# Expert rows of two groups scattered into one PSUM tile and added once; the crowded branch moved ahead of the last rounding

## Chip, cores and metric

The kernel runs on one core of one Trainium2 chip. The metric is the device time of one launch in microseconds (us); the kernel before was run three times: 2159.14, 2161.22 and 2164.48 us, a median of 2161.22.

## The reference, cut to what matters

The program is one step of a four-layer transformer trunk on 384 tokens (128 context, 256 latent) of width 1024. Each layer has a token mixer (gated delta rule, grouped-query attention, latent attention, gated delta rule), a layer norm, a mixture of experts, and a layer norm. The change is in the mixture of experts alone:

```python
scores = sigmoid(t @ router_w); sel = scores + router_b
best_group = argmax(sum of the two best sel of each group of 4)    # 4 groups of 4 experts
e_idx = the two best experts within best_group; w = scores at e_idx, divided by their sum
hid = silu(t @ w_gate[e]) * (t @ w_up[e])                          # 256 wide, 16 experts
out = sum over e of (hid * combine[:, e]) @ w_down[e]
x   = layer_norm(ALPHA * x + (1 + gate) * out)
```

Each token uses experts of one group only. All is float32.

## The kernel before, in words

**Tiling.** A group's tokens are gathered into a tile of 128 rows by a matmul with a 0/1 matrix (`e_pick`), its four experts are computed on this tile, and the result (128 rows of 1024) is put back to the 384 token positions by a matmul with another 0/1 matrix (`e_put`), feature tile by feature tile: eight tiles (`ft` 0 to 7) of 128 features by 384 tokens. If any group has more than 128 tokens, the rest is computed in extra blocks behind a branch on a flag (`flags[0:1, 0, 2:3]`); with these inputs that arm isn't run, but each of TensorE, VectorE and ScalarE loads the flag and branches once per layer.

**Precision.** Float32 products are made of rounded parts (float32r): ScalarE copies a weight piece to a rounded `e_whi` (`split_high`, by L1722), VectorE subtracts to get the remainder `e_wlo` (`split_low`, L2857), and TensorE runs three matmuls per product: hi by hi, hi by lo, lo by hi (`split_products`, L1515, L1518, L1519). Expert weights stream from HBM in units of 1 MB into a ring of eight; a unit is two pieces, an expert six pieces (four gate and up, two down). The split parts have three buffers (`SPLITS`).

**The plan.** `MOE_STEPS` is the order on TensorE, written out once and used in each layer: for x = 0 to 15 the steps U(x), the gate and up products of expert x; D(x-2), the down product of expert x-2, which accumulates a group's four experts in PSUM banks 3 and 4; T(x-1), the transposes of its hidden rows (bank 2); and at some x the gathers G of the second pair of groups, the pair's weights W, and the scatters S. `MOE_FOLLOW` is derived from it: the order in which ScalarE and VectorE follow (P is the splits of a piece, u the silu and product of U, t the transposed hidden rows' rounding, y the rounding of a finished group's rows, s the additions of a scatter). A step's work on ScalarE and VectorE is placed behind the splits of the second piece of the next U or D.

**Scatter and addition.** When group j is done, ScalarE rounds its rows into `e_yhi` and VectorE makes the remainder `e_ylo` (`y_high`, `y_low`, L2870), in two halves. A step S(j, q) is two feature tiles (`scatter_piece`): each is two matmuls of 128x384 into one PSUM bank (L1545 with `e_yhi`, L1546 with `e_ylo`), and then VectorE adds the tile, times the gate, into the residual `bufx` (`scattered`, L2876) in two instructions, one for the 128 context columns and one for the 256 latent ones. Per layer: 4 groups x 8 tiles x 2 = 64 matmuls and 64 additions. The four steps of groups 0, 1 and 2 are in the plan at x = 6 and 7, 10 and 11, 14 and 15, two at each x; those of group 3 come last, behind D of the last expert. Banks 5 and 6 take turns for groups 0 to 2; group 3 has 6, 0, 1, 2. A tile's matmuls wait until the bank's last tile is added. `put_back(j)` (L2834) makes the 0/1 matrix of group j in one of two buffers; it runs for groups 2 and 3 after the additions of groups 0 and 1.

**The branch.** Before the last group's scatter each engine runs `crowded_blocks`: load the flag (L1564 on TensorE, L2173 on ScalarE, L2882 on VectorE), compare and branch (L1565, L2174, L2884), and in the arm taken here only increments of semaphores (from L1597, L2207, L2916), which stand for the blocks left out. On ScalarE and VectorE that is behind the rounding of group 3; on TensorE it is behind its last down product. Then TensorE scatters, VectorE adds, and the column sums of the layer norm (L812) follow the additions tile by tile.

`bufh` holds the mixer's and experts' input; in the expert stage its first 1024 columns are free unless a block of a crowded group uses them, the next 1024 hold `e_sg` and `e_hid`, and the last 1024 are free.

## Time and profile before

| What | Value |
|---|---|
| median of three runs | 2161.22 us |
| profiled execution | 2164.33 us, its span 2162.5 us |
| TensorE matmuls busy | 2007.7 us, 93% |
| VectorE busy | 1335.3 us, 62% |
| ScalarE busy | 1027.7 us, 48% |
| `e_wlo` split on VectorE (L2857) | 384 of 1220 ns |
| additions into `bufx` on VectorE (L2876) | 256 of 408 ns |

In the views, PE is TensorE's matmuls and PEld its weight loads, DVE is VectorE, ACT ScalarE, SP the queue that issues the loads; a q behind the name is the engine's sequencer. A row of a timeline gives the start in us, the duration in us, engine, line, operation, the tiles written and read, and in brackets how long the engine was idle before it and what ended that; adjacent instructions of one kind are merged with their count. A row by stretch gives the stretch, its length, the busy us (and the number of instructions) of PE, PEld, DVE, ACT and POOL, then TensorE's mean granted clock as a share of full speed, the DMA share and GB/s. Matmuls overlap: one of 128x384 reads 0.34 us, and the next starts 0.17 to 0.18 us after it.

### The profile page before, as it was taken

Reading aid. Unit: us, or ns where it says so; the run is one execution under the profiler, and the core shown is the slowest. Engines: PE = TensorE matmul, PEld = TensorE weight load, DVE = VectorE, ACT = ScalarE, POOL = GpSimd, SP = SyncE. Lnnn points to the kernel's source line nnn. Section 1 sums busy time; section 2 is a strip of 40 time slices with the busy share of each in tenths; the row PEclk is TensorE's granted clock in tenths of the full one; section 3 lists DMA queues with packets and bytes.
Section 4 is the critical chain, followed back from the end, with each engine's and each line's share of the span. In section 5 each row is a group of like instructions: output and inputs, shape, how many; then the busy total and the mean of one; then the engine's idle time right before and its main releaser. Section 6 shows DMA issues by size and latency. Waiting matters only on the chain.

```text
span 2162.5 us, 45013 instructions
## 1 busy us (share of the span) xinstructions
PE 2007.7 (93%) x18880; PEld 1401.7 (65%) x18881; DVE 1335.3 (62%) x2625; ACT 1027.7 (48%) x1779; POOL 246.4 (11%) x363
## 2 busy tenths in 40 slices
PE   6999999899998999899899999998999999989996
PEld 3666666557775675687665666776566666646774
DVE  2666666448895341789722326898666666538896
ACT  3344344227773340676523315766444444327774
POOL 1422222110001000100010001000322232100000
PEclk9999999999999999999999999999999999999999
DMA  9244333257885244788632356888311121125880
GB/s 396 90 160 149 123 131 136 107 184 284 287 315 190 98 169 158 263 305 302 225 109 101 117 198 232 300 304 293 113 53 66 46 70 46 46 81 188 282 308 31
DMA packets 56911, 381.21 MB, mean 176 GB/s; under 512 B 6400, under 2 KB 10624, under 8 KB 12144
## 3 DMA queue, kind: packets, MB, share of 16 engines
q1 hardware_dynamic: 51696, 373.00, 48.3%
q10 hardware_dynamic: 4608, 4.20, 0.6%
q8 instruction: 158, 2.59, 0.5%
q0 software_dynamic: 384, 0.89, 0.1%
q14 instruction: 65, 0.53, 0.1%
HBM read 373.96 MB, written 4.10 MB: 175 GB/s over the span
## 4 chain that ended last, share of the span: by engine, by line
PE 74%; DVE 16%; ACT 5%; issue 3%; DMA 1%; DVEq 0%; SPq 0%; ACTq 0%
PE ps L851 15%; DVE e_wlo L2857 7%; PE ps L1515 5%; PE ps L1519 5%; PE ps L1518 5%; PE ps L801 4%; PE ps L777 4%; PE ps L757 4%; PE ps L1304 3%; PE ps L992 3%; DVE bufx L2876 3%; PE ps L812 2%; PE ps L1471 2%; ACT e_whi L1722 2%; PE ps L1404 2%
## 5 line engine op out<-in xcount | busy, mean ns | idle before, releaser
L2857 DVE TENSOR_TENSOR e_wlo<-ring,e_whi 128x1024 fp32r<-128x1024 f32 x384 | 455.0, 1220 | 70.1 <-ACT e_whi L1722 68.6
L1722 ACT ACTIVATE e_whi<-ring 128x1024 fp32r<-128x1024 f32 x384 | 402.5, 1060 | 114.7 <-PE ps L1519 111.9
L851 PE MATMUL ps<-bufh,ring 128*128 128x384 f32 x1024 | 390.2, 503 | 2.0 <-ACT scratch L1722 0.6
L1515 PE MATMUL ps<-e_whi,e_hs 128*128 128x512 f32 x512 | 211.1, 412 | 35.7 <-DVE e_wlo L2857 32.5
L851 PEld LDWEIGHTS ps<-bufh,ring 128*128 128x128 f32 x1024 | 176.2, 190 | 92.6 <-issue 16.4
L1722 ACT ACTIVATE scratch<-ps 128x384 f32<-128x384 f32 (+6 forms) x311 | 109.1, 368 | 214.3 <-PE ps L851 53.0
L1519 PE MATMUL ps<-e_whi,e_hs 128*128 128x512 f32 x512 | 200.7, 392 | 0.0
L1518 PE MATMUL ps<-e_wlo,e_hs 128*128 128x512 f32 x512 | 200.1, 391 | 0.0
L2994 POOL TENSOR_SCALAR bufx<-bufo,x_gb 128x384 f32<-128x384 f32 x56 | 37.6, 686 | 1065.8 <-DVE bufo L2294 1065.8
L1515 PEld LDWEIGHTS ps<-e_whi,e_hs 128*128 128x128 f32 x512 | 96.2, 188 | 77.6 <-ACT e_whi L1722 52.2
L2389 DVE SCALAR_TENSOR_TENSOR scratch<-scratch,par 128x386 f32<-128x386 f32 x192 | 128.4, 669 | 4.8
L757 PE MATMUL ps<-ring,silc 128*32 128x128 f32 x3072 | 110.7, 295 | 17.0 <-DMA ring<-in_w_ada 17.0
L1722 ACT ACTIVATE scratch<-ps,scratch 128x128 f32<-128x128 f32 x96 | 31.7, 364 | 190.3 <-PE ps L1152 188.7
L757 PEld LDWEIGHTS ps<-ring,silc 128*32 128x32 f32 x3072 | 91.5, 119 | 31.2 <-issue 14.8
L1519 PEld LDWEIGHTS ps<-e_whi,e_hs 128*128 128x128 f32 x512 | 96.2, 188 | 21.5
L1518 PEld LDWEIGHTS ps<-e_wlo,e_hs 128*128 128x128 f32 x512 | 96.6, 189 | 16.3
L1515 PE MATMUL ps<-e_whi,e_hidT 128*128 128x512 f32 x256 | 101.1, 395 | 3.2 <-DVE e_wlo L2857 3.2
L1722 ACT ACTIVATE lnt<-ps 128x384 f32<-128x384 f32 x26 | 12.7, 489 | 192.2 <-PE ps L812 176.0
L1518 PE MATMUL ps<-e_wlo,e_hidT 128*128 128x512 f32 x256 | 100.5, 392 | 0.0
L1519 PE MATMUL ps<-e_whi,e_hidT 128*128 128x512 f32 x256 | 100.1, 391 | 0.0
L992 PEld LDWEIGHTS ps<-scratch 32*32 32x32 f32 x6144 | 64.5, 107 | 50.9 <-issue 36.2
L2876 DVE SCALAR_TENSOR_TENSOR bufx<-ps,mod,bufx 128x128 f32<-128x128 f32 (+1 forms) x256 | 87.6, 408 | 15.0 <-DVEq L2922 8.5
(311 smaller groups left out, 3416.1 us busy)
## 6 DMA issues: line engine op xcount, KB each, us to landing
ring<-in_moe SPq DMA_DIRECT2D x192, 1024.0 KB, 4.9
ring<-in_w_ada SPq DMA_DIRECT2D x96, 1024.0 KB, 5.5
ring<-in_gdn_w_in SPq DMA_DIRECT2D x32, 1024.0 KB, 6.9
ring<-in_gdn_w_out SPq DMA_DIRECT2D x8, 1024.0 KB, 5.0
ring<-in_gqa_w_in SPq DMA_DIRECT2D x6, 1024.0 KB, 5.0
ring<-in_gqa_w_out SPq DMA_DIRECT2D x4, 1024.0 KB, 6.9
ring<-in_mla_w_out SPq DMA_DIRECT2D x4, 1024.0 KB, 8.1
ring<-in_mla_w_in SPq DMA_DIRECT2D x3, 1024.0 KB, 5.0
```

Of the source, the lines that this page charges most:

```text
L757: last = mm(ps[32 * g:32 * g + 32, bank, 0:P], silc[:, kt, :], w[:, k, g, :], start=(kt == 0), stop=(kt == KT - 1))
L777: last = mm(ps[:, banks[t % len(banks)], 0:T], w[:, t % 2, kt, :], rhs[:, kt, :], start=(kt == 0), stop=(kt == KT - 1))
L801: last = mm(ps[:, banks[t % len(banks)], 0:T], w[:, t % 2, kt, :], bufo[:, kt, :], start=(kt == 0), stop=(kt == KT - 1))
L851: last = mm(ps[:, head_bank(n, m), 0:T], w[:, m % 2, kt, :], bufh[:, kt, :], start=(kt == 0), stop=(kt == KT - 1))
L992: last = mm(ps[quarter(g), bank, at:at + 32], g_inv[a][quarter(g), d, t, :], g_inv[b][quarter(g), d, t, :], start=True, stop=True)
L1515: first = mm(out, parts[0], whi, start=start, stop=False)
L1518: mm(out, parts[0], wlo, start=False, stop=False)
L1519: return mm(out, parts[1], whi, start=False, stop=stop)
L1722: return op(out, in_, ACT.Copy, **kw)
L2389: done = stt(acc, g_cin[:, m, tap:tap + CONVW], taps[:, tap:tap + 1], acc, ALU.mult, ALU.add)
L2857: return tt_(e_wlo[:, b, :], w, e_whi[:, b, :].bitcast(F32), ALU.subtract)
L2876: last = stt(bufx[:, ft, cols], ps[:, banks[ft % len(banks)], cols], mrow(l, 5, ft, seg), bufx[:, ft, cols], ALU.mult, ALU.add)
```

## The change

- Groups 0 and 1 are scattered together, and so are 2 and 3: the four matmuls of a feature tile (two parts of each group) accumulate in one bank, and VectorE adds the tile once (`scatter_pair`, `group_rows`). For that the rows of the odd group lie in `bufh_r`, the same memory as `bufh` under another type, beside `e_yhi` and `e_ylo`.
- In the plan, the scatter of groups 0 and 1 is one step of two feature tiles at each of x = 10, 11, 12 and 13. The scatters at x = 6, 7, 14 and 15 go. At x = 15 a new step A puts group 2's part of the first four feature tiles into banks 6, 7, 0 and 1 (`third_group_rows`, eight matmuls); no additions go with it. The rest follows behind the last down product, with five banks (6, 7, 0, 1, 2): group 3's part of tiles 0 to 3, both groups' parts of tiles 4 to 7.
- Both `put_back` of groups 2 and 3 run after the last addition of the first pair.
- The flag is loaded before the last down product (TensorE) or behind the last t (ScalarE and VectorE). The branch comes behind D of the last expert on TensorE and behind the last split on the other two, ahead of `y_high` and `y_low` of group 3, and both arms begin with this group's work; the increments come after it.
- Counts of waits on `sc_ev` are halved, and VectorE waits for its own `hid` ahead of the second pair's weights.

The diff, cut to its core:

```diff
 for _x in range(NE):
-    _group, _turn = divmod(_x - 6, EPG)
-    _late = _x >= 6 and _turn < 2
...
         MOE_STEPS.append(("T", NG - 1, EPG - 2))
-    if _late:
-        MOE_STEPS.append(("S", _group, 2 * _turn))
+    if 10 <= _x < 14:
+        MOE_STEPS.append(("S", 1, _x - 10))
     if _x >= 2:
         MOE_STEPS.append(("D", (_x - 2) // EPG, (_x - 2) % EPG))
...
     if _x == NE - 1:
-        MOE_STEPS.append(("T", NG - 1, EPG - 1))
-    if _late:
-        MOE_STEPS.append(("S", _group, 2 * _turn + 1))
+        MOE_STEPS += [("T", NG - 1, EPG - 1), ("A", NG - 1, 0)]
     if 1 <= _x < NE - 1:
         MOE_STEPS.append(("T", (_x - 1) // EPG, (_x - 1) % EPG))
 MOE_STEPS += [("D", 3, 2), ("D", 3, 3)] + [("S", 3, q) for q in range(4)]
...
                 _open = []
+    if _kind == "A":
+        continue
...
 HS_OF = [0, 1, 0, 2]
+LAST_BANKS = (6, 7, 0, 1, 2)
+EARLY_ROWS = 4
...
-        bufh = sb("bufh", [P, KT, T])
+        with nc.sbuf_tensor("bufh", [P, KT, T], F32) as bufh:
+            pass
+        bufh_r = sb("bufh_r", [P, KT, T], F32R).rearrange("p k t -> p (k t)")
...
         e_yhi, e_ylo = sb("e_yhi", [P, D], F32R), sb("e_ylo", [P, D], F32R)
+        y_parts = [(e_yhi, e_ylo), (bufh_r[:, 0:D], bufh_r[:, 2 * D:3 * D])]
...
+
+            def group_rows(l, j, ft, b):
+
+                for part in range(2):
+                    last = mm(ps[:, b, 0:T], y_parts[j % 2][part][:, P * ft:P * ft + P], e_put[:, j % 2, :],
+                              start=(j % 2 == 0 and part == 0), stop=(j % 2 == 1 and part == 1))
+                return last
+
+            def scatter_pair(l, j, ft, banks, begun):
+
+                n, b = 2 * l + j // 2, banks[ft % len(banks)]
+                if ft >= len(banks):
+                    pe.wait_ge(F["sc_ev"], n * KT + (ft - len(banks) + 1))
+                elif n:
+                    pe.wait_ge(F["sc_ev"], n * KT)
+                if not begun:
+                    group_rows(l, j - 1, ft, b)
+                if ft % 4 == 0:
+                    pe.wait_ge(F["yhi"], 2 * (NG * l + j) + ft // 4 + 1)
+                    pe.wait_ge(F["ylo"], 2 * (NG * l + j) + ft // 4 + 1)
+                group_rows(l, j, ft, b).then_inc(F["sc"], 1)
+
+            def third_group_rows(l):
+
+                pe.wait_ge(F["yhi"], 2 * (NG * l + NG - 1))
+                pe.wait_ge(F["ylo"], 2 * (NG * l + NG - 1))
+                pe.wait_ge(F["sc_ev"], KT * (2 * l + 1))
+                for ft in range(EARLY_ROWS):
+                    group_rows(l, NG - 2, ft, LAST_BANKS[ft])
...
-                crowded = pe.value_load(flags[0:1, 0, 2:3], min_val=0, max_val=1)
+            def last_scatter(l):
+
+                for ft in range(KT):
+                    scatter_pair(l, NG - 1, ft, LAST_BANKS, ft < EARLY_ROWS)
+
+            def last_group(l, comb, crowded):
+
                 with pe.If(crowded > 0):
-                    pe.wait_ge(F["yhi"], 2 * NG * (l + 1))
-                    pe.wait_ge(F["ylo"], 2 * NG * (l + 1))
-                    pe.wait_ge(F["sc_ev"], KT * (NG * (l + 1) - 1))
+                    last_scatter(l)
+                    pe.wait_ge(F["sc_ev"], KT * 2 * (l + 1))
...
                 with pe.Else():
+                    last_scatter(l)
                     pe.sem_inc(X["ga"], BLOCKS * 5)
...
                         pe.wait_ge(F["tlo"], n + 1)
+                        if j == NG - 1 and e == EPG - 1:
+                            pe.wait_ge(flags_ready, l + 1)
+                            crowded = pe.value_load(flags[0:1, 0, 2:3], min_val=0, max_val=1)
                         for k in range(2):
                             p = MOE_PIECE_OF["D", j, e, k]
                             down(F, MOE_PIECES * l + p, p, e, k)
-                    else:
-                        n = NG * l + j
+                    elif kind == "A":
+                        third_group_rows(l)
+                    elif j == 1:
                         if e == 0:
-                            if j == NG - 1:
-                                crowded_blocks(l, comb)
                             pe.wait_ge(F["ga_ev"], 16 * l + 16)
-                        scatter_piece(F, n, e, e_put[:, j % 2, :], (6, 0, 1, 2) if j == NG - 1 else (5, 6),
-                                      n * KT if n else None)
+                            pe.wait_ge(F["yhi"], 2 * (NG * l + 1))
+                            pe.wait_ge(F["ylo"], 2 * (NG * l + 1))
+                        for ft in (2 * e, 2 * e + 1):
+                            scatter_pair(l, 1, ft, (5, 6), False)
+                last_group(l, comb, crowded)
...
-                layer_norm(2 * l + 1, bufx, bufh, lambda k: pe.wait_ge(F["sc_ev"], KT * (NG * l + NG - 1) + k + 1),
...
-            def y_high(S, used_pieces):
+            def y_high(S, used_pieces, hi):
                 act.wait_ge(S["wfree"], used_pieces)
                 for y in range(2):
-                    copy((e_yhi if S is F else x_yhi)[:, 512 * y:512 * y + 512], ps[:, 3 + y, :]).then_inc(S["yhi"], 1)
+                    copy(hi[:, 512 * y:512 * y + 512], ps[:, 3 + y, :]).then_inc(S["yhi"], 1)
...
-                    elif kind == "y":
-                        y_high(F, before + MOE_PIECE_OF["D", j, e, 1] + 1)
-                act.wait_ge(flags_ready, l + 1)
-                crowded = act.value_load(flags[0:1, 0, 2:3], min_val=0, max_val=1)
+                    elif kind == "y" and j < NG - 1:
+                        y_high(F, before + MOE_PIECE_OF["D", j, e, 1] + 1, y_parts[j % 2][0])
+                    if kind == "t" and (j, e) == (NG - 1, EPG - 1):
+                        act.wait_ge(flags_ready, l + 1)
+                        crowded = act.value_load(flags[0:1, 0, 2:3], min_val=0, max_val=1)
                 with act.If(crowded > 0):
+                    y_high(F, MOE_PIECES * (l + 1) + SPLITS, y_parts[1][0])
                     with act.Fori(0, NG) as g:
...
                 with act.Else():
+                    y_high(F, MOE_PIECES * (l + 1) + SPLITS, y_parts[1][0])
                     act.sem_inc(X["ga_ev"], BLOCKS * 4)
...
-                    dve.wait_ge(F["sc_ev"], KT * NG * (n // 2 + 1))
+                    dve.wait_ge(F["sc_ev"], KT * 2 * (n // 2 + 1))
...
-            def y_low(S, n):
+            def y_low(S, n, hi, lo):
                 for y in range(2):
                     dve.wait_ge(S["yhi"], 2 * n + y + 1)
                     cols = slice(512 * y, 512 * y + 512)
-                    hi, lo = (e_yhi, e_ylo) if S is F else (x_yhi, x_ylo)
...
-                crowded = dve.value_load(flags[0:1, 0, 2:3], min_val=0, max_val=1)
+            def last_additions(l):
+
+                y_low(F, NG * l + NG - 1, *y_parts[1])
+                dve.wait_ge(F["sc_ev"], KT * (2 * l + 1))
+                for q in range(4):
+                    scattered(F, l, 2 * l + 1, q, LAST_BANKS)
+
+            def last_group(l, crowded):
+
                 before_all = (v.base, v.n)
                 with dve.If(crowded > 0):
+                    last_additions(l)
                     with dve.Fori(0, NG) as g:
...
                 with dve.Else():
+                    last_additions(l)
                     dve.sem_inc(chain_v, v.n - before_all[1])
...
                     elif kind == "w":
+                        if j:
+                            dve.wait_ge(F["hid"], NE * l + 2 * EPG)
                         pair_weights(l, j)
...
-                    elif kind == "y":
-                        y_low(F, NG * l + j)
-                    elif kind == "s":
-                        if e == 0 and j == NG - 1:
-                            crowded_blocks(l)
-                        if e == 0 and l + j:
-                            dve.wait_ge(F["sc_ev"], KT * (NG * l + j))
-                        scattered(F, l, NG * l + j, e, (6, 0, 1, 2) if j == NG - 1 else (5, 6))
-                        if e == 3 and j < 2:
-                            put_back(j + 2)
+                    elif kind == "y" and j < NG - 1:
+                        y_low(F, NG * l + j, *y_parts[j % 2])
+                    elif kind == "s" and j == 1:
+                        if e == 0 and l:
+                            dve.wait_ge(F["sc_ev"], KT * 2 * l)
+                        scattered(F, l, 2 * l, e, (5, 6))
+                        if e == 3:
+                            put_back(2)
+                            put_back(3)
+                    if kind == "t" and (j, e) == (NG - 1, EPG - 1):
+                        dve.wait_ge(flags_ready, l + 1)
+                        crowded = dve.value_load(flags[0:1, 0, 2:3], min_val=0, max_val=1)
+                last_group(l, crowded)
```

## Rows read from the trace of the kernel before

**Rows 1.** The page: engines of the chain that ended last; weight loads, KB, us to landing.

```profile
PE 74%; DVE 16%; ACT 5%; issue 3%; DMA 1%; DVEq 0%; SPq 0%; ACTq 0%
...
ring<-in_moe SPq DMA_DIRECT2D x192, 1024.0 KB, 4.9
```

**Rows 2.** Busy time by stretch: turns of layer 0, then the joint of layer 1.

```profile
516.38:525.12 8.74, 8.73 (x38) 6.81 (x39) 7.90 (x9) 6.92 (x8) 0.00 (x0) 1.00 0.97 357
557.64:568.49 10.85, 10.11 (x47) 8.28 (x47) 10.32 (x17) 7.57 (x9) 0.00 (x0) 1.00 0.86 293
568.49:580.66 12.17, 11.47 (x58) 9.61 (x59) 10.80 (x19) 6.86 (x9) 0.00 (x0) 1.00 0.77 258
609.80:620.99 11.19, 10.15 (x47) 8.29 (x47) 10.56 (x18) 7.23 (x9) 0.00 (x0) 1.00 0.88 289
620.99:629.75 8.76, 8.76 (x39) 6.83 (x39) 7.82 (x9) 5.97 (x8) 0.00 (x0) 1.00 0.89 335
629.75:639.28 9.53, 8.74 (x39) 6.79 (x39) 9.02 (x11) 8.29 (x11) 0.00 (x0) 1.00 0.99 348
650.12:661.30 11.18, 10.39 (x49) 8.46 (x49) 10.56 (x18) 6.56 (x9) 0.00 (x0) 1.00 0.84 284
1062.62:1075.75 13.13, 8.57 (x32) 5.43 (x32) 6.58 (x18) 2.57 (x4) 0.00 (x0) 0.61 0.22 79
```

**Rows 3.** VectorE's timeline in turn 11: start, us, instruction, count, idle time before.

```profile
617.67 1.38 DVE L2876 SCALAR_TENSOR_TENSOR bufx<-ps,mod,bufx 128x128 f32<-128x128 f32 x4
618.97 0.41 DVE L2834 TENSOR_SCALAR e_put<-lnt,con 128x384 fp32r<-128x384 f32 x1
```

**Rows 4.** Timelines of ScalarE and VectorE around the four joints.

```profile
664.30 1.08 ACT L1722 ACTIVATE e_yhi<-ps 128x512 fp32r<-128x512 f32 x2 [4.06 <-PE ps L1519]
664.93 1.29 DVE L2870 TENSOR_TENSOR e_ylo<-ps,e_yhi 128x512 fp32r<-128x512 f32 x2 [2.64 <-ACT e_yhi L1722]
...
670.26 5.29 DVE L2876 SCALAR_TENSOR_TENSOR bufx<-ps,mod,bufx 128x128 f32<-128x128 f32 x16 [4.04 <-PE ps L1546]
...
1069.19 5.29 DVE L2876 SCALAR_TENSOR_TENSOR bufx<-ps,mod,bufx 128x128 f32<-128x128 f32 x16 [4.62 <-DVEq L2922]
...
1513.71 5.29 DVE L2876 SCALAR_TENSOR_TENSOR bufx<-ps,mod,bufx 128x128 f32<-128x128 f32 x16 [3.85 <-DVEq L2922]
...
2135.94 5.29 DVE L2876 SCALAR_TENSOR_TENSOR bufx<-ps,mod,bufx 128x128 f32<-128x128 f32 x16 [2.39 <-PE ps L1546]
```

**Rows 5.** TensorE's timeline: the first scatter matmuls of the four joints.

```profile
669.14 0.65 PE L1545 MATMUL ps<-e_put,e_yhi 128*128 128x384 f32 x1 [4.88 <-issue]
669.59 0.52 PE L1546 MATMUL ps<-e_put,e_ylo 128*128 128x384 f32 x1
669.91 0.52 PE L1545 MATMUL ps<-e_put,e_yhi 128*128 128x384 f32 x1
...
1066.05 0.66 PE L1545 MATMUL ps<-e_put,e_yhi 128*128 128x384 f32 x1 [3.43 <-issue]
...
1511.05 0.41 PE L1545 MATMUL ps<-e_put,e_yhi 128*128 128x384 f32 x1 [3.15 <-issue]
...
2135.21 0.41 PE L1545 MATMUL ps<-e_put,e_yhi 128*128 128x384 f32 x1 [3.61 <-issue]
```

**Rows 6.** Sequencer instructions: count, ns min/median/max, first and last start in us.

```profile
L1564 PEldq TENSOR_LOAD <-flags x4: 303/306/488, 662.5 to 2129.8; - x4
...
L1565 PEldq COMPARE_BRANCH  x4: 3392/3770/4949, 663.3 to 2130.4; - x4
...
L2174 ACTq COMPARE_BRANCH  x4: 45/48/54, 665.1 to 2132.2; - x4
...
L2207 ACTq EVENT_SEMAPHORE  x4: 17/17/17, 669.0 to 2135.0; - x4
...
L2884 DVEq COMPARE_BRANCH  x4: 56/63/67, 666.3 to 2133.4; - x4
...
L2916 DVEq EVENT_SEMAPHORE  x4: 21/21/21, 669.3 to 2133.9; - x4
```

More of the change, by code:

```diff
@@ L1531, in down, with scatter_block @@
                 last.then_inc(S["wfree"], 1)
-            def scatter_piece(S, n, q, put, banks, first_of_two):
+            def scatter_block(n, q):
                 for ft in (2 * q, 2 * q + 1):
                     if ft % 4 == 0:
-                        pe.wait_ge(S["yhi"], 2 * n + ft // 4 + 1)
-                        pe.wait_ge(S["ylo"], 2 * n + ft // 4 + 1)
-                    if ft >= len(banks):
-                        pe.wait_ge(S["sc_ev"], n * KT + (ft - len(banks) + 1))
-                    elif first_of_two is not None:
-                        pe.wait_ge(S["sc_ev"], first_of_two)
-                    b = banks[ft % len(banks)]
-                    hi, lo = (e_yhi, e_ylo) if S is F else (x_yhi, x_ylo)
-                    mm(ps[:, b, 0:T], hi[:, P * ft:P * ft + P], put, start=True, stop=False)
-                    mm(ps[:, b, 0:T], lo[:, P * ft:P * ft + P], put,
-                       start=False, stop=True).then_inc(S["sc"], 1)
+                        pe.wait_ge(X["yhi"], 2 * n + ft // 4 + 1)
+                        pe.wait_ge(X["ylo"], 2 * n + ft // 4 + 1)
+                    if ft >= 2:
+                        pe.wait_ge(X["sc_ev"], n * KT + (ft - 2 + 1))
+                    b = (5, 6)[ft % 2]
+                    mm(ps[:, b, 0:T], x_yhi[:, P * ft:P * ft + P], x_put, start=True, stop=False)
+                    mm(ps[:, b, 0:T], x_ylo[:, P * ft:P * ft + P], x_put,
+                       start=False, stop=True).then_inc(X["sc"], 1)
@@ L1587, in crowded_blocks @@
                                 for q in range(4):
-                                    scatter_piece(X, n, q, x_put, (5, 6), None)
+                                    scatter_block(n, q)
                                 pe.wait_ge(X["sc_ev"], n * KT + KT)
@@ L1711, in _ @@
                 moe(l)
-                layer_norm(2 * l + 1, bufx, bufh, lambda k: pe.wait_ge(F["sc_ev"], KT * (NG * l + NG - 1) + k + 1),
+                layer_norm(2 * l + 1, bufx, bufh, lambda k: pe.wait_ge(F["sc_ev"], KT * (2 * l + 1) + k + 1),
                            ("tail", l) if l + 1 < DEPTH else None)
@@ L2900, in crowded_blocks @@
                                         split_low(X, n * (EPG * PIECES) + p, p, spare[:, 0:PIECE]).then_inc(X["wlo"], 1)
-                                y_low(X, n)
+                                y_low(X, n, x_yhi, x_ylo)
                                 for q in range(4):
```

6 lines of the change are left out of this document (1 added, 5 removed).

## The prediction

> **What bounds the kernel now.** I read the chain of waits first [rows 1]: 74% of it is TensorE, 16% VectorE. Then I cut one expert stage into "turns", from one matmul that starts on a fresh `e_wlo` to the same one of the next expert. Turn x holds the gate and up products of expert x, the down products of expert x-2 and what the plan hangs between them. The four stages repeat each other's turns to 0.1 us; seven turns of layer 0 stand in [rows 2]. A plain turn is TensorE's own work (8.73 busy of 8.74 us; turn 12, which begins at 620.99, is one too). Turn 6, with two scatter steps (557.64), lasts 10.85 us and TensorE is busy for 10.11 of it: eight scatter matmuls cost 10.11 - 8.73 = 1.38 us (0.17 each), and 0.74 us is idle. VectorE is busy for 10.3 to 10.6 us of such turns, 7.9 in a plain one: here the two engines bind together. Turns 10 and 14 are like turn 6. Turn 7 (568.49, with the weights product of a pair), 11 (609.80) and 15 (650.12) are idle for 0.70, 1.04 and 0.79 us. A turn in which a group's rows are rounded (9, 13; 629.75) takes 9.53, of which 0.79 idle.
>
> The second place is the joint behind the last down product ("D33"), four times. TensorE's idle time before its first scatter matmul is 4.88, 3.43, 3.15, 3.61 us [rows 5], so D33 ended at 664.26, 1062.62, 1507.90 and 2131.60. VectorE's first addition comes 6.00, 6.57, 5.81 and 4.34 us after these [rows 4]. The rounding is done in 2.0 us (from 664.26 to 664.93 + 1.29 [rows 4]); the rest is the branch. TensorE's compare-and-branch itself lasts 3.4 to 4.9 us. On VectorE and ScalarE it takes about 0.05 us, but the next instruction comes 3.0 us (layer 0) and 0.5 us (layer 3), or 3.9 and 2.8 us, after it [rows 6].
>
> **The expert stage, turn by turn.** The scatter matmuls stay 64 per layer, 40 of them now in the stage (before 48): eight each in turns 10 to 13 and 15. The additions fall from 64 to 32 per layer, in the stage from 48 to 16; four cost 1.38 us on VectorE [rows 3].
> - Turns 6 and 14 become plain: 10.85 to 8.74, -2.1 each.
> - Turn 7 keeps the weights product: TensorE's 11.47 less 1.38 is 10.1; I allow 10.3: -1.9.
> - Turns 10 and 11: TensorE 10.15, VectorE 10.3 less 1.38, about 8.9. The cover is now 1.2 us thick, and I count their idle time as gone: -0.7 and -1.0.
> - Turn 12: 8.76 to 10.15, VectorE 7.8 plus 1.4: +1.4.
> - Turn 13 gets the scatter on top of a rounding, and both mask comparisons that turns 7 and 11 had (0.41 us each [rows 3]). VectorE: 9.0 + 1.4 + 0.8 = 11.2; I take that: +1.7.
> - Turn 15: no additions, matmuls as before: 11.18 to 10.4, -0.8. The flag load that VectorE now takes ahead of its last two splits (TensorE's own needs 0.6 to 0.8 us from load to branch [rows 6]) lies in the 2.8 us that its additions leave. TensorE's load comes while the matmuls of the down product before are still queued.
>
> Sum: -5.5 us per layer, four layers **-22.0**. The wait for `hid` that VectorE gets ahead of the pair's weights is on its own work of three splits earlier: nothing. Reading the second y tile from `bufh` has the same shape: nothing. Bounds: if each scatter turn keeps its idle time, one turn's worth goes, -2.1 per layer, -8.4. If the rounding turns' 0.8 went too, it would be -29.
>
> Turns get denser in bytes. A plain turn moves 357 GB/s with a DMA share of 0.97 [rows 2], which looks full. But the row shown is one of several that run back to back near the start of the stage with TensorE never idle, and a unit lands in 4.9 us [rows 1] with eight in the ring. No turn asks for more after the change. I count transfers at nothing.
>
> **The joint.** Times here are from D33's end. ScalarE is free at 664.30 - 4.06, that is at -4.0, and a pause of 3.9 ends there in time. VectorE is free at 664.93 - 2.64, that is at -2.0 [rows 4]; with pauses of 0.5 to 4 us (4 for layer 1, whose idle time was 0.6 longer than layer 0's) its first half of `lo` starts at +0.7 to +2.1 and is ready at +1.3 to +2.8. TensorE issued its branch at -1.0 and -1.2 (663.3, 2130.4); without the load (0.8) at -1.8; with 3.4 to 4.9 us that ends at +1.6 to +3.2. Between the branch's end (663.3 + 4.95) and the first matmul lie 0.9 us, four increments above all, which come after the scatters now; I keep 0.25. First scatter matmul: +3.4, +2.8, +2.0, +2.3; first addition 0.8 later: +4.3, +3.6, +2.8, +3.1. Against today's: -1.7, -3.0, -3.0, -1.2, in all -8.9. Then 16 additions run for 5.3 us as before. TensorE has 24 matmuls there instead of 16 (four rows need two, four need four): at 0.17 each 4.2 us, covered by the additions. At 1.2 GHz they are 0.32 apart (from 669.59 to 669.91) [rows 5], 7.7 us, and TensorE is the bound: up to +2.1 in a layer. Layer 1's joint ran at a mean granted clock of 0.61 [rows 2], mostly the lower of the two levels, after its idle time. Less idle time makes that rarer, not impossible; I take 0.8 us in three layers, +2.4. The joint: **-6.5**, between -10 and +1.
>
> The row of the branch on VectorE is 0.06 us long, and the pause comes behind it. The Trainium skill (Advanced Engine Details and Errata, Control Flow Timing) gives about 108 ns for a compare-and-branch; by that alone, as an estimate, four moved branches are worth 0.4 us and the sum would be some 6 us smaller. Its page Runtime: NRT & Kernel Launch (Instruction fetch mechanics) says that a taken branch out of the prefetched stretch waits for a fetch; the rows' 0.5 to 3.9 us agree with this one.
>
> **Sum.** -22.0 - 6.5 = -28.5. The profiled execution took 2164.33 us (span 2162.5), 3.1 above the median of 2161.22; taken from the median that gives **2132.7 us**.
>
> **Rivals.**
> - *The scatter turns keep their idle time*: it comes from the hand-over of splits and transposes, not from VectorE's load. For it: VectorE has 0.5 us idle there too. Against: plain turns with the same hand-overs have none. -8.4 - 6.5: 2146. Chance 0.13.
> - *The joint gives nothing back*: TensorE at half clock in all four, 24 matmuls as the bound (-8.9 + 8.4), or pauses that no move hides because they count from D33's end. For it: layer 1's clock. Against: layer 3's full clock after 3.61 us idle (its first matmul is a short one). 2139, or 2141 if the joint loses a little. Chance 0.12.
> - *Transfers bind*: if the 290 GB/s of the scatter turns were the most that lasts, the stage keeps its length and only the joint gains: 2155. Against: the plain turns. 0.06 for no change, 0.01 for a small gain.
> - *Slower: the pause behind the branch grows.* The rounding lies behind it now, so a pause that the idle time doesn't cover delays ScalarE, VectorE and TensorE in turn. It has to push the first addition 7.1 us beyond the forecast's, to 10.6 us after D33's end, to eat all gains: a pause of 11 us on VectorE or TensorE, 12 on ScalarE. The longest seen is 4.9. With 13 us: 2170. Chance 0.04.
>
> The forecast holds with 0.64, its own range 2124 to 2141. A measurement of this kernel tells 0.3% (6.5 us) from no change. Faster: 0.64 + 0.13 + 0.12 + 0.01 = 0.90; within: 0.06; slower: 0.04. Eight times in ten: 2122 to 2149, which takes in the clock, the kept idle time and a joint at its best.
>
> **What would show it.** Right: turns 6 and 14 at 8.7 us, 10 to 12 near 10.15, 13 near 11.2; 128 additions instead of 256; first addition 2.8 to 4.3 us after D33; TensorE's branch begun 1.8 us before D33's end and still 3 to 5 us long. Wrong: scatter turns of 10.8 us with VectorE idle; waits on the ring; a granted clock near 0.5 in the joints with VectorE waiting for TensorE between additions; ScalarE's `hi` copy starting more than 1 us after D33.

## The result and the profile after

| What | Before | After |
|---|---|---|
| median | 2160.77 us (4 runs, 2159.14 to 2164.48) | 2137.18 us (4 runs, 2134.62 to 2140.15) |
| ratio after / before, 95% interval | | 0.9893, 0.9874 to 0.9912 |
| profiled execution | 2164.33 us, span 2162.5 | 2139.05 us, span 2137.2 |

The kernel is 23.6 us faster by the medians, 25.3 by the two profiled executions; forecast were 28.5. I cut both traces alike: "stage" from the first transpose of a layer's expert turns to the end of the last down product (D33), "joint" from there to the mean of the next layer norm on ScalarE, and all the rest "outside". "Sum of four" adds the four layers.

| us, sum of four | before | after | difference | forecast |
|---|---|---|---|---|
| stages | 604.6 | 580.3 | -24.3 | -22.0 |
| joints | 48.0 | 43.3 | -4.6 | -6.5 |
| outside | 1509.9 | 1513.6 | +3.6 | 0 |

The page of the kernel after, its chain that ended last, against [rows 1]:

```profile
PE 84%; DVE 9%; ACT 4%; issue 2%; DMA 1%; SPq 0%; DVEq 0%; ACTq 0%
...
ring<-in_moe SPq DMA_DIRECT2D x192, 1024.0 KB, 4.9
```

VectorE's share of the chain fell from 16% to 9%. That is some 150 us by the two shares, far more than the 25 us gained: the chain tells through which engine it runs, not what was saved. Weights still land in 4.9 us. Busy time by stretch, kernel after, layer 0: turns 6, 7, 11, 13 and 15, with the columns of [rows 2]:

```profile
555.36:564.10 8.74, 8.74 (x38) 6.79 (x39) 7.90 (x9) 6.92 (x8) 0.00 (x0) 1.00 0.94 346
564.10:573.98 9.88, 9.88 (x51) 8.28 (x51) 7.98 (x10) 6.91 (x8) 0.00 (x0) 1.00 0.88 321
602.44:612.61 10.17, 10.17 (x46) 8.26 (x47) 9.20 (x13) 6.91 (x8) 0.00 (x0) 1.00 0.89 310
622.75:634.14 11.39, 10.34 (x46) 8.29 (x47) 10.87 (x17) 8.49 (x11) 0.00 (x0) 1.00 0.88 291
642.87:653.04 10.17, 10.17 (x49) 8.59 (x49) 8.13 (x10) 7.29 (x9) 0.00 (x0) 1.00 0.87 316
```

In each of these turns but 13 TensorE is busy for the whole stretch. Turn 11 has eight scatter matmuls and no idle time, with VectorE at 9.20 of 10.17 us; before it lasted 11.19 us, with TensorE at 10.15 and VectorE at 10.56 (609.80 in [rows 2]). Turn 13, which carries rounding, scatter and masks, is the one that VectorE still sets.

The joints, VectorE's timeline of the kernel after; the number in brackets is the idle time before the row. These answer to [rows 4]:

```profile
658.94 1.29 DVE L2909 TENSOR_TENSOR bufh_r<-ps,bufh_r 128x512 fp32r<-128x512 f32 x2 [4.75 <-issue]
...
1052.06 1.29 DVE L2909 TENSOR_TENSOR bufh_r<-ps,bufh_r 128x512 fp32r<-128x512 f32 x2 [4.67 <-issue]
...
1489.30 1.29 DVE L2909 TENSOR_TENSOR bufh_r<-ps,bufh_r 128x512 fp32r<-128x512 f32 x2 [4.17 <-issue]
1491.29 5.57 DVE L2915 SCALAR_TENSOR_TENSOR bufx<-ps,mod,bufx 128x128 f32<-128x128 f32 x16 [0.70 <-PE ps L1552]
...
2107.24 1.29 DVE L2909 TENSOR_TENSOR bufh_r<-ps,bufh_r 128x512 fp32r<-128x512 f32 x2 [2.43 <-ACT bufh_r L1759]
2109.86 5.29 DVE L2915 SCALAR_TENSOR_TENSOR bufx<-ps,mod,bufx 128x128 f32<-128x128 f32 x16 [1.33 <-PE ps L1552]
```

D33 ends at 655.96, 1049.14, 1486.90 and 2106.57. VectorE has nothing to do from 1.8 us before that. In the fourth layer it waits 2.43 us for ScalarE's high part (the rounded copy `hi`), as it must; in the first three the wait is 4.2 to 4.8 us and is put down to "issue": the profile shows nothing in the program that holds it. So the low part (the remainder `lo`) starts at +2.98, +2.91, +2.40 and +0.67 us. TensorE's first scatter matmuls and its branch, against [rows 5] and [rows 6]:

```profile
659.77 0.41 PE L1552 MATMUL ps<-e_put,bufh_r 128*128 128x384 f32 x1 [3.82 <-DVE bufh_r L2909]
...
1052.89 2.77 PE L1552 MATMUL ps<-e_put,bufh_r 128*128 128x384 f32 x8 [3.75 <-DVE bufh_r L2909]
...
1490.20 1.30 PE L1552 MATMUL ps<-e_put,bufh_r 128*128 128x384 f32 x3 [3.30 <-DVE bufh_r L2909]
...
2109.17 1.11 PE L1552 MATMUL ps<-e_put,bufh_r 128*128 128x384 f32 x5 [2.59 <-DVE bufh_r L2909]
```

```profile
L1597 PEldq COMPARE_BRANCH  x4: 4023/4328/4738, 654.4 to 2105.0; - x4
L2929 DVEq COMPARE_BRANCH  x4: 62/63/72, 653.0 to 2103.6; - x4
```

The bracket names VectorE as releaser in all four, but read the branch beside it. It begins 1.6 us before D33's end and lasts 4.0 to 4.7: in the fourth layer it ends 2.42 us after D33 and the matmul follows at +2.59, long after the low part's first half. There the branch ended the wait, and in the third layer too (+3.14 against +3.30); in the first two VectorE did. The first addition starts at +4.51, +4.71, +4.39 and +3.29.

### The profile page after: what moved, and what is told of

Same layout as the page of the kernel before. It is cut to its first block, busy times and chain, and to the rows that moved or that the text cites. A ratio compares the mean times of both kernels' runs of the same rounds, so it can differ in the third digit from the quotient of the medians.

```text
span 2137.2 us, 44861 instructions
## 1 busy us (share of the span) xinstructions
PE 2006.5 (94%) x18880; PEld 1402.0 (66%) x18881; DVE 1301.4 (61%) x2497; ACT 1028.5 (48%) x1779; POOL 246.2 (12%) x363
## 4 chain that ended last, share of the span: by engine, by line
PE 84%; DVE 9%; ACT 4%; issue 2%; DMA 1%; SPq 0%; DVEq 0%; ACTq 0%
PE ps L854 15%; PE ps L1518 8%; PE ps L1522 7%; PE ps L1521 7%; PE ps L804 4%; PE ps L780 4%; PE ps L760 4%; PE ps L1307 3%; PE ps L995 3%; DVE e_wlo L2897 3%; PE ps L1552 2%; PE ps L1474 2%; PE ps L815 2%; PE ps L1407 2%; PE ps L1376 2%
## 5 line engine op out<-in xcount | busy, mean ns | idle before, releaser
L2313 DVE SCALAR_TENSOR_TENSOR bufh<-ps,mod,bufx 128x128 f32<-128x128 f32 x64 | 23.4, 412 | 118.9 <-PE ps L780 77.3
```

## Experiments

Joint figures are from the profiled execution of each kernel. "First matmul" is the first scatter matmul after D33's end.

**Each half of the change alone.** Pairs of groups, with load and branch where they were:

```diff
-                        if j == NG - 1 and e == EPG - 1:
-                            pe.wait_ge(flags_ready, l + 1)
-                            crowded = pe.value_load(flags[0:1, 0, 2:3], min_val=0, max_val=1)
...
+                pe.wait_ge(flags_ready, l + 1)
+                crowded = pe.value_load(flags[0:1, 0, 2:3], min_val=0, max_val=1)
                 last_group(l, comb, crowded)
...
-                    elif kind == "y" and j < NG - 1:
+                    elif kind == "y":
```

and likewise on the other two engines.

> The pairing and the new plan alone; flag load and branch stay behind the rounding on ScalarE and VectorE and behind the last down product on TensorE. If the sum by parts holds, the expert stage gives all it gave in the changed kernel (143.5 us from the first transposes to the last become 137.8, in four layers 23 us) and the joint gives nothing: first addition about 5.7 us after D33's end, as before, 24 matmuls instead of 16, time 2137 to 2142. Rival, that the branch's move gave the larger part: time 2146 or more.

Measured: 2141.88 us (ratio 0.9896, 0.9864 to 0.9928). Stages 580.5, joints 51.0, 3.0 more than before. The first matmul comes at +5.49, +4.42, +5.21, +3.10, although the low part starts at +0.67 in every layer. The first additions (+6.58, +5.51, +6.29, +4.74) are only 0.4 us later in sum than before; the 3.0 us lie behind them, where the 16 additions take 6.44, 5.51, 5.96 and 6.22 us instead of 5.29, with 24 matmuls to wait for and TensorE at the lower of its two clock levels for 6.8, 3.4, 6.8 and 6.8 us of the joints. TensorE's timeline:

```profile
660.29 1.62 PE L1552 MATMUL ps<-e_put,bufh_r 128*128 128x384 f32 x4 [5.49 <-issue]
```

The branch alone, on the kernel before: rounding and last scatters inside both arms, load and branch ahead.

```diff
-                    elif kind == "y":
+                    elif kind == "y" and j < NG - 1:
                         y_low(F, NG * l + j)
...
+            def last_additions(l):
+
+                y_low(F, NG * l + NG - 1)
+                dve.wait_ge(F["sc_ev"], KT * (NG * l + NG - 1))
+                for q in range(4):
+                    scattered(F, l, NG * l + NG - 1, q, (6, 0, 1, 2))
...
                 with dve.Else():
+                    last_additions(l)
```

> The moved branch alone, with the old plan and an addition for each group. By the traces' sum: the stage keeps 143.5 us from first to last transposes; the first addition comes 4.4 us after D33's end instead of 5.7, so -5 to -6 us in all, time 2154 to 2156. Rival, that VectorE's longer pause gives it all back: 2159 to 2162.

Measured: 2152.0 us (0.9949, 0.9931 to 0.9967). Stages 604.8 as before; joints 37.9, which is 10.1 less than before and 5.4 less than in the whole change. That is below the 2154 to 2156 that I expected: the first additions come at +3.50, +3.87, +2.75 and +2.89, and not at +4.4. So the stage's gain belongs to the pairs and the joint's to the branch, but the two parts do not add: with pairs, the joint keeps only 4.6 of the 10.1 us. Of the 5.4 us between this kernel and the change, 3.9 are first additions that come later, and the rest is additions that take longer. VectorE's timeline of this kernel ahead of its low part in the first layer (D33 ends at 661.75), and that of the whole change (655.96):

```profile
657.40 2.35 DVE L2864 TENSOR_TENSOR e_wlo<-ring,e_whi 128x1024 fp32r<-128x1024 f32 x2
663.76 0.69 DVE L2877 TENSOR_TENSOR e_ylo<-ps,e_yhi 128x512 fp32r<-128x512 f32 x1 [4.01 <-ACT e_yhi L1726]
```

```profile
650.98 1.23 DVE L2897 TENSOR_TENSOR e_wlo<-ring,e_whi 128x1024 fp32r<-128x1024 f32 x1 [0.77 <-ACT e_whi L1759]
652.96 1.23 DVE L2897 TENSOR_TENSOR e_wlo<-ring,e_whi 128x1024 fp32r<-128x1024 f32 x1 [0.76 <-ACT e_whi L1759]
```

On the old stage VectorE is late: the two last splits run back to back, and its sequencer takes the branch while the first of them runs, at 657.7, 4.1 us before D33's end. With pairs VectorE is early and waits for each split's input, so the branch comes behind the last wait, at 653.0, 3.0 us before D33's end. From branch to low part it is 6.1 us in the one and 6.0 in the other. The pairs did not lengthen this step; they let it begin 1.1 us later, measured from D33, and the low part starts 1.0, 0.8, 1.1 and 0.0 us later. TensorE's own branch adds to that: 4.0 to 4.7 us in the change, 3.6 to 3.8 here. The additions take longer by TensorE's work: 24 matmuls instead of 16, at the lower clock level the bound of the additions.

**No branch at all.** Left out are the flag load, the branch and the arm for crowded groups on all three engines; the straight arm stands in line.

```diff
-                with pe.If(crowded > 0):
...
-                with pe.Else():
-                    last_scatter(l)
-                    pe.sem_inc(X["ga"], BLOCKS * 5)
+                last_scatter(l)
+                pe.sem_inc(X["ga"], BLOCKS * 5)
```

> The changed kernel without the arm for crowded groups, without flag load and branch (that part of the computation is left out; these inputs don't use it). It prices what is left of the branch. If the branch alone delays the joint: first scatter matmul 1.5 to 1.7 us after D33's end (rounding of the first half), first addition 0.8 later, against 4.2 in the changed kernel: -1.9 per layer, -7 to -8 in all, 2127 to 2131. Rival, that another path (rounding, the clock) sets the joint: less than 3 us gained.

Measured: 2128.5 us (0.9843, 0.9801 to 0.9885). Joints 33.7, the same to 0.01 us in all four layers: low part at +0.67, first matmul at +1.50, first addition at +2.20. They are 9.6 us shorter than the change's, more than the 7 to 8 expected, because the additions take 5.29 us here in every layer. Timelines of TensorE and then VectorE, layer 0:

```profile
659.10 1.63 PE L1552 MATMUL ps<-e_put,bufh_r 128*128 128x384 f32 x8 [1.50 <-DVE bufh_r L2844]
```

```profile
658.26 1.29 DVE L2844 TENSOR_TENSOR bufh_r<-ps,bufh_r 128x512 fp32r<-128x512 f32 x2 [2.43 <-ACT bufh_r L1728]
659.79 5.29 DVE L2850 SCALAR_TENSOR_TENSOR bufx<-ps,mod,bufx 128x128 f32<-128x128 f32 x16 [0.24 <-PE ps L1552]
```

2.43 us is what VectorE's wait is without a branch, so in the change the branch adds 2.3, 2.2, 1.7 and 0.0 us there. All that was not the same from layer to layer in the joints is gone with the branch.

**Why not the fourth layer?** The one thing that it lacks is a next layer whose weights are on their way. Busy time by stretch from 3 us before D33's end to 2 after it, second and fourth layer of the kernel after; the last two columns are the DMA share and GB/s:

```profile
1046.14:1051.14 5.00, 3.00 (x14) 2.05 (x12) 1.23 (x1) 1.94 (x3) 0.00 (x0) 1.00 0.99 324
2103.57:2108.57 5.00, 3.00 (x14) 2.05 (x12) 2.51 (x3) 1.94 (x3) 0.00 (x0) 1.00 0.03 10
```

The same second layer's stretch by DMA queue: packets, MB, share of the 16 engines.

```profile
q1 hardware_dynamic: 209, 1.58, 96.6%
q8 instruction: 1, 0.02, 1.2%
q14 instruction: 3, 0.02, 1.2%
```

Four packets of kind "instruction" travel on the engines that 209 weight packets keep full. That gave the theory: the pause is the fetch of the branch's target, and the fetch shares the DMA engines with the loads. (Which engine fetches by which queue, the trace doesn't say.) The experiment holds the loads, and nothing else, over that stretch:

```diff
                 if u >= RING:
                     used(sp, u - RING)
+                for l in range(DEPTH - 1):
+                    if u == unit_at["moe", l] + len(MOE_UNITS) + RING - 3:
+                        sp.wait_ge(F["ylo"], 2 * NG * (l + 1) - 1)
```

> The changed kernel with the loads of the next stage held back from about 5 us before D33's end until VectorE has the first half of the last remainder, so that few transfers run while the three engines branch. Theory A, that the pause behind the branch is a fetch which shares the DMA engines with the weights: VectorE's pause falls from 4.2 to 4.7 us of idle time to 3 or less in layers 0 to 2, as in layer 3, first addition 0.7 to 1.2 us earlier, -2 to -4 us. Theory B, that the pause hangs on where the branch's target lies in the instruction stream and not on traffic: VectorE's idle time stays within 0.3 us, time the same or a little longer by the delayed loads.

Measured: 2132.37 us (0.9866, 0.9816 to 0.9916). The second layer by stretch and by DMA queue, VectorE's timeline and TensorE's branch, all of this kernel:

```profile
1041.76:1046.76 5.00, 3.00 (x14) 2.05 (x12) 2.52 (x3) 1.94 (x3) 0.00 (x0) 1.00 0.03 8
```

```profile
q14 instruction: 3, 0.02, 1.5%
q8 instruction: 1, 0.02, 1.3%
```

```profile
1045.43 1.29 DVE L2912 TENSOR_TENSOR bufh_r<-ps,bufh_r 128x512 fp32r<-128x512 f32 x2 [2.43 <-ACT bufh_r L1762]
```

```profile
L1600 PEldq COMPARE_BRANCH  x4: 3402/3486/3548, 651.7 to 2100.5; - x4
```

There are four instruction packets again, alone now. They come earlier, too. In the 3.26 us that end with the second layer's D33, queue q14 has, in the change and then with the held loads:

```profile
q14 instruction: 1, 0.01, 0.8%
```

```profile
q14 instruction: 3, 0.02, 2.3%
```

In the change three more start only in the 1.1 us behind D33, together with that of q8. The packets' own share is as small beside the loads as without them (1.2% and 1.5% for three of them above); what grows is the time until the next one starts. Whether they wait in the DMA engines or at the memory, these runs don't separate.

VectorE's longer pause is gone in all layers: 2.43 us and released by ScalarE, so that what is left of the fetch is hidden behind that wait. TensorE's branch lasts 3.4 to 3.5 us instead of 4.0 to 4.7; but the fourth layer, without loads in both kernels, has 3.5 and 4.0, so not all of this is the loads. First matmul +1.96, +2.15, +2.01, +2.12; joints 37.5 against 43.3, stages 580.5. The time outside is 1513.8 us against 1513.6; by the last experiment it varies by several us between executions, so a small loss by the held loads would not be seen.

**The reverse.** If transfers make the pause, the fourth layer must get it when it gets transfers:

```diff
                 if l < DEPTH - 1:
                     ada_stage("tail", l)
+            for x in range(RING - 1):
+                load(I["w_ada"][x], n_units + x)
```

> The changed kernel with seven more weight loads queued behind those of the last layer, into ring slots that nobody reads again, so that the last layer's joint has the transfers that the other three have and that it lacks. Theory (the fetch behind VectorE's branch waits on the DMA engines): in the fourth layer y_low moves from +0.67 to +2.2 to +3.2 us behind the last product and VectorE's pause from 2.4 to some 4 to 5 us, the first scatter product from +2.3 or +2.6 to +3.0 to +4.0; the other layers stay. Rival (the fourth layer is quick because its branch's target lies elsewhere in the program, or because the layer was laid out otherwise): +0.67 stays.

Measured: 2143.5 us, one run. Fourth layer by stretch (3 us before D33's end to 2 after), and VectorE's timeline there:

```profile
2106.78:2111.78 5.00, 3.00 (x14) 2.05 (x12) 1.23 (x1) 1.94 (x3) 0.00 (x0) 1.00 0.62 216
```

```profile
2112.01 1.29 DVE L2911 TENSOR_TENSOR bufh_r<-ps,bufh_r 128x512 fp32r<-128x512 f32 x2 [3.98 <-issue]
```

The low part moved from +0.67 to +2.22, the pause from 2.43 to 3.98, and "issue" stands in place of ScalarE; first matmul at +3.14. The branch stands at the same place of the program; only the load queue got seven more loads. Taken and given, the pause follows the loads.

**The held loads again, the change again, and the hold on the kernel before,** on one chip in one series.

> The kernel with the held loads again, beside the changed kernel on the same chip. Theory (the fetch behind VectorE's branch shares the DMA engines with the next stage's loads): y_low starts at +0.7 us behind the last product in every layer, joints 36 to 39 us, 2130 to 2134, some 4 to 6 us below the changed kernel. Rival (the first run's 2132.4 was an execution's luck): within 2 us of the changed kernel.

> The changed kernel as it is. Theory: joints 42 to 45 us, stages 580.3; the segments outside the stages differ from run to run by some microseconds (the stretch between the third and the fourth layer's stage was 460.5 before and 463.7 after), so this run's may lie anywhere between 1510 and 1515. Rival (the new program is laid out so that the mixers are slower by 3 to 4 us): 463 to 464 for that stretch and 1513 to 1514 for all again, while the kernel before stays at 460.5.

Measured: with held loads 2131.51 us (5 runs, ratio 0.9852, 0.9829 to 0.9876), the change 2138.19 us (6 runs, 0.9879, 0.9854 to 0.9904); 6.7 us apart by the medians, with intervals that overlap; the joints, which repeat better, are 4.9 us apart here and were 5.8 apart in the first series. The change's joints sum to 43.6 and its low part starts at +2.52, +2.93, +2.40, +0.66: the pauses repeat. With held loads: 38.7, and +0.66 or +0.67 four times; TensorE's branch takes 3.4 to 3.9 us there. The change's time outside was 1516.7, above the 1510 to 1515 that I expected.

On the kernel before, released by the first scatter matmul of the last group:

```diff
+                for l in range(DEPTH - 1):
+                    if u == unit_at["moe", l] + len(MOE_UNITS) + RING - 3:
+                        sp.wait_ge(F["sc"], KT * (NG * (l + 1) - 1) + 1)
```

> The kernel before, with the next stage's loads held until the first scatter product of a layer's last group. Theory (TensorE's branch behind the last product also fetches through the DMA engines, and part of its 3.15 to 4.88 us is contention with the loads): first scatter product at 2.0 to 3.3 us after the last product in all four layers, joints 42 to 45 us against 48.0, 2154 to 2157. Rival (only VectorE's and ScalarE's fetches, begun while loads run, are slowed; TensorE's has its length anyway, or the release only moves the loads into the mixer): joints within 1.5 us of 48.0, or the joints' gain comes back as more time outside the stages, 2159 to 2162.

Measured: 2157.77 us (0.9981, 0.9967 to 0.9996), joints 45.3. A gain of about 4 us (the interval allows 1 to 7), of which the joints show 2.7, but not as the theory had it. First matmul at +3.54, +3.96, +4.09, +3.12, later than the 2.0 to 3.3 expected:

```profile
L1568 PEldq COMPARE_BRANCH  x4: 3370/3886/4261, 660.5 to 2118.1; - x4
```

TensorE's branch has a length of its own of 3.4 us or more, with loads or without. Its median is 3.9 us here and was 3.5 and 3.6 in the two executions with held loads. The three engines' branches stand about equally close in both kernels (TensorE -1.0, ScalarE +0.6, VectorE +1.8 us here; ScalarE -4.1, VectorE -3.0, TensorE -1.6 in the changed kernel), so their distance doesn't explain it; whether the fetches hinder each other, or the order counts, was not tried.

**What set the scatter turns?** The turns lost additions and changed their order at once. This kernel puts VectorE's work back and nothing else, a copy behind each of the first pair's additions:

```diff
                                    bufx[:, ft, cols], ALU.mult, ALU.add)
+                    if S is F and n % 2 == 0:
+                        for cols in (CTXS, LATS):
+                            last = V.tensor_copy(e_hi.rearrange("p t d -> p (t d)")[:, T * ft:T * ft + T][:, cols],
+                                                 ps[:, banks[ft % len(banks)], cols])
                     last.then_inc(S["sc_ev"], 1)
```

> The changed kernel with VectorE's work in the four scatter turns put back to what it was: behind each addition of the first pair stands a copy of the same PSUM columns into a tile that nobody reads (16 more operations a layer, about 0.34 us each as the additions, so 1.4 us more a turn); TensorE's work is untouched. Theory (before, these turns were set by VectorE, and the change gained by halving its additions): turns 10 to 13 return from 10.15 us (8.74 and 8 matmuls of 0.176) to 10.6 to 10.9, the stages cost 2 to 3 us more a layer, span 2145 to 2150. Rival (the turns were slow because of scatter matmuls that waited on banks and split operands, and the new order of the matmuls cured that): turns stay at 10.15, span 2137 give or take 3.

Measured: 2148.62 us, one run. Stages 591.7, 2.85 more a layer than the change. Turns 11 and 13 of layer 0 by stretch:

```profile
606.45:617.22 10.77, 10.16 (x47) 8.30 (x46) 10.16 (x17) 6.92 (x8) 0.00 (x0) 1.00 0.84 292
...
627.97:640.34 12.37, 10.28 (x47) 8.13 (x46) 12.08 (x21) 8.60 (x11) 0.00 (x0) 1.00 0.79 268
```

Turns 10 to 12 are 10.85, 10.77 and 10.75 us again (10.17, 10.17 and 10.14 in the change), with TensorE's work about unchanged at 10.16 (10.24 in turn 10) and its idle time of 0.6 us back. The copies also hold each PSUM bank longer, so the rival of waits on banks has to be looked for in the rows. TensorE's one wait in turn 11 of this kernel, and the one at the end of turn 11 of the kernel before:

```profile
614.37 0.47 PE L1518 MATMUL ps<-e_whi,e_hs 128*128 128x512 f32 x1 [0.61 <-DVE e_wlo L2897]
```

```profile
609.80 0.47 PE L1515 MATMUL ps<-e_whi,e_hs 128*128 128x512 f32 x1 [0.73 <-DVE e_wlo L2857]
```

Both wait for a split by VectorE, none for a bank. The idle time of these turns came with VectorE's additions. Turn 13 went to 12.37, beyond the range I gave for all four, because it was VectorE's already at 11.39.

**The kernel before once more,** for the time outside.

> The kernel before, profiled once more. Theory (the mixers are the same in both kernels and differ only by how long TensorE's clock stood at its lower level in them): outside the stages it lies on the same line as all runs so far, the stretch between the third and fourth layer's stage at 457.3 to 470.7 us for 17 to 37 us of half clock in it; joints 46 to 50 us, first scatter product 3 to 5 us behind the last product. Rival (the old program has faster mixers): that stretch is 460.5 again with over 25 us of half clock in it, or below 458.

Measured: 2155.75 us, one run; stages 604.5, joints 47.0, outside 1502.4, which is 7.5 us less than in the first execution of the same program. The joints and the stretch below came out in the ranges given. So what lies outside varies by more than the +3.6 that I had to explain. The largest segment of it is the one between the third and the fourth layer's joint and stage. Busy time by stretch for it: kernel before, its second execution, the change, its second execution.

```profile
1519.92:1980.41 460.49, 437.42 (x5710) 281.91 (x5711) 284.10 (x639) 201.93 (x427) 104.90 (x151) 0.98 0.20 68
```

```profile
1511.48:1971.12 459.64, 437.90 (x5710) 281.19 (x5711) 284.21 (x639) 201.88 (x427) 104.95 (x151) 0.98 0.20 68
```

```profile
1497.78:1961.48 463.70, 439.16 (x5710) 282.67 (x5711) 284.25 (x639) 201.93 (x427) 104.90 (x151) 0.97 0.20 67
```

```profile
1494.75:1965.48 470.73, 446.52 (x5710) 289.02 (x5711) 284.39 (x639) 202.25 (x427) 104.91 (x151) 0.96 0.20 66
```

The same 5710 matmuls, the same work on VectorE to 0.3 us; what differs is TensorE's busy time and its granted clock. The trace has TensorE at the lower of its two levels for 20.5, 20.5, 23.9 and 37.5 us of these stretches. Over all twelve profiled executions the segment goes from 457.3 us with 17 us at the lower level to 470.9 with 37.5, but not on one line: the kernel with the branch moved alone has 463.3 with the 20.5 us of the kernel before's 460.5. Over all that lies outside stages and joints, the lower level adds up to 76.8 and 56.8 us in the two executions of the kernel before (1509.9 and 1502.4 us in all) and to 84.1 and 94.2 in those of the change (1513.6 and 1516.7).

## Why the prediction was right, and where it was off

**The stage: right, turn by turn.** Turns 6 and 14 came out at 8.74 and 8.73 (8.74 forecast), 10 to 12 at 10.17, 10.17 and 10.14 (10.15), 13 at 11.39 (11.2), 7 at 9.88 (10.3), 15 at 10.17 (10.4). The last two were taken too long by 0.4 and 0.2 us. In turn 7, 0.2 us is idle time that I left in; the rest is TensorE's busy time, which came out 0.2 us shorter in each of the two than I read it from the old turns (turn 15: 10.39 us before and 10.17 now, with 49 matmuls in both). Why, the runs don't say. That is most of the missing 0.6 us a layer; -24.3 came for -22.0. The sentence "the cover is now 1.2 us thick, and I count their idle time as gone" is the one on which 0.7 and 1.0 us per layer hung; the turns with the work put back show it. The rival in which the idle time stays is excluded by turns 10 to 12, which have none, and the one of binding transfers by turn 6, which moves 346 GB/s now, where 290 was to be the most.

**The joint: right in kind, mis-sized in one term.** The first additions were forecast at +4.3, +3.6, +2.8, +3.1 and came at +4.51, +4.71, +4.39, +3.29: 5.8 us gained against 8.9. The term is VectorE's pause behind its branch. The step that failed reads "VectorE is free at 664.93 - 2.64, that is at -2.0" and goes on "with pauses of 0.5 to 4 us" to a first half of `lo` that "starts at +0.7 to +2.1". The low part came at +2.98, +2.91 and +2.40 in the three layers that load. I carried the pause of the old place (3.0, 4.0, 3.3 and 0.5 us from the branch to the next instruction) to the new one as if it were a property of the branch. It grows with the transfers beside it, and the old place was the quieter one: over these pauses the DMA share was 0.38, 0.33, 0.40 and 0.04; at the new place it is 0.98 in the three layers that load, and there the same step takes 5.96, 5.89 and 5.38 us. That the fetch begins at -3.0 and not at -2.0 gave 1 us of it back. For the branch moved alone the forecast's numbers would have held (low parts at +2.01, +2.08, +1.26 and +0.67), but by luck: the step is as long there (6.1, 6.1 and 5.3 us), and it begins at -4.1, while VectorE is still busy. So the second half of the miss is that I let the fetch begin when VectorE is free, and priced the two parts apart: the pairs took away VectorE's lateness, which had hidden the fetch's first 2 us.

TensorE's branch began 1.6 us before D33's end (1.8 forecast) and took 4.0 to 4.7 us (3.4 to 4.9). ScalarE had no delay: its high part starts 0.04 us after D33's end in all layers. The term of the clock was +2.4; the additions took 6.06, 5.80, 5.57 and 5.29 us, +1.6 over before. Stages and joints together came to -28.9 where -28.5 was forecast: that is partly luck, since the stages gave 2.3 us more and the joints 1.9 less.

The Trainium skill's 108 ns for a compare-and-branch (Advanced Engine Details and Errata, Control Flow Timing) is contradicted by these rows for a branch whose target has to be fetched: 3.4 us at the least on TensorE. What its page Runtime: NRT & Kernel Launch says under Instruction fetch mechanics, that a sequencer fetches through a DMA queue of its own and that a taken branch to elsewhere waits for that, agrees with the packets of kind "instruction" on queues apart from the weights' (q8 and q14 against q1) and with the held loads. That such a fetch competes with weight loads, and by how much, is from the runs.

**The rivals.** "The joint gives nothing back" is wrong in its mechanism: the clock was lower for 3.4 us in each of three joints, not through all of them. "Slower: the pause grows" named what happened, far below the size it needed: the first addition came 0.2, 1.1, 1.6 and 0.2 us later than forecast, where 7.1 would have eaten the gains.

**Outside: a term that the sum lacked.** By the two profiled executions it was +3.6 us. The clock explains it in part. Over all of it the lower level lasts 7.3 us longer after the change, which at half speed is worth up to 3.7 us, the whole of it. But in the largest segment it lasts 3.4 us longer, worth 1.7 us; TensorE's busy time grew by 1.7, the segment by 3.2. Between the two executions with held loads the time outside differs by 6.0 us (1513.8 and 1507.8) with only 3.3 us more at the lower level, so the clock isn't all there either. That the three executions with the old turns and the old branch have 457.3 to 460.5 us in the largest segment and the nine others 462.9 to 470.9 (463.3 with the branch moved alone) suggests, and no more, that it isn't chance between the two. Whether a shorter joint shifts the clock's low stretches in the mixer behind it, or something else does, stays open: no run holds the phase of the clock. With stages and joints at -28.9 and the medians at -23.6, about 5 us went there. This term is as large as the forecast's whole miss of 4.9 us.

**What beats both.** The change with held loads: 2131.5 and 2132.4 us in two series. Without any branch the time is 2128.5, and the joints are 33.7 us against 37.5 and 38.7, so the branch still costs some 4 to 5 us.

## What to carry to other kernels

A branch whose target has to be fetched isn't free, though its row may be only 0.06 us long: read the idle time marked "issue" behind it, and the DMA share of the microseconds around it. If the loads that run there aren't needed at once, hold them for the length of the fetch; here one wait on the load queue took 5 to 6 us out of the joints. And where two engines bind together in a repeated turn, taking work from the one shows its full value only up to the other's busy time, which the view by stretch gives to 0.1 us.

## What the runs showed of the hardware

- The pause behind a branch on VectorE is about twice as long beside weight loads: 2.8 to 3.0 us to the next instruction with the loads held (kernel before, first three layers, DMA share 0.05 or less), 5.3 to 6.1 us with a DMA share of 0.88 to 0.98 (the change, and the branch moved alone). On ScalarE it is 2.5 to 2.6 us held, and 4.0 to 5.0 in the first three layers of the kernel before.
- The loads are not all: in the kernel before this step was 0.53 us in the fourth layer, in both executions and with the loads held, and 2.89 us there in the kernel with pairs only, all with a quiet DMA. Why was not tried.
- TensorE's compare-and-branch lasts 3.4 to 4.3 us with a DMA share of 0.06 or less, and 3.4 to 6.1 us with one of 0.6 or more. In the change it is 4.2 to 4.7 us beside loads and 3.4 to 4.0 without them (the fourth layer, and the loads held); but the kernel before had 3.39 and 3.67 us at a share of 0.81 and 0.84, and the branch moved alone 3.6 to 3.8 at 0.88. So the loads alone don't set its length; what else does is open.
- Of the same program, the time outside stages and joints differed by 7.5 us between two executions (1509.9 and 1502.4), with TensorE's clock at its lower level for 76.8 and 56.8 us of it.
